# A hybrid decoder step: projection and heads in one block, a PSUM copy between two chunks, the output projection by seven products

## What is computed

```python
qa, ka, va, qb, kc, vc, ksl, vsl, kw, vw, gates = _mix_inputs(xp, norm_attn[l], w_in[l])   # RMSNorm, one projection
o_a = _dilated_prompt(qa, ka, va, bias_a)                  # 8 heads, windows (128,1), (512,4), (2048,16)
o_cmp, p_slc = _nsa_compressed(qb, _compress(kc, *cmp_k), _compress(vc, *cmp_v), pos_p, bias_b)
top_i, top_ok = _nsa_select(p_slc, pos_p)                  # 16 blocks of 64 tokens
o_slc = _nsa_selected_prompt(qb, ksl, vsl, top_i, top_ok, pos_p, bias_b)
o_win, _ = _banded_attention(qb, kw, vw, NSA_WINDOW, 1, bias_b)
o_b = _gate_branches(gates, o_cmp, o_slc, o_win)
xp, conv_p = _out_and_ffn(xp, o_a, o_b, *ffn_w, ...)       # output projection + residual, RMSNorm, up, conv, SiLU gate, down
```

## Time and profile before

| what | value |
|---|---|
| median of three runs | 2149.1 us (2150.56, 2148.54, 2149.1) |
| the profiled execution | 2152.93 us, its span 2151.2 us |
| mean granted clock of TensorE | 0.981 |
| busy PE, DVE, ACT, POOL | 2051.5, 1082.9, 521.6, 532.7 us |
| `front` | 0 to 508 us |
| `compressed_and_dilated` | 512.5 to 627 |
| `sample_selected` | 635.5 to 832 |
| `prompt_attention` | 835.6 to 1180.3 |
| `ffn`: output projection, up, down | 1182 to 1307.9, to 1864.7, to 2145 |

### The profile page before, as it was taken

One profiled execution on the slowest core, in us unless ns is written; L12 is line 12 of the kernel. 1 busy time (PEld: TensorE's weight loads), 2 busy tenths in 40 slices (PEclk: granted clock), 3 DMA queues, 4 the chain that ended last, 5 costly groups with the idle time before them and its releaser, 6 DMA issues. The chain is left out here.

```text
span 2151.2 us, 31682 instructions
## 1 busy us (share of the span) xinstructions
PE 2051.5 (95%) x12366; PEld 1339.3 (62%) x12366; DVE 1082.9 (50%) x2484; ACT 521.6 (24%) x1106; POOL 532.7 (25%) x714
## 2 busy tenths in 40 slices
PE   6999999998977997999999999999999999999998
PEld 3445466665545665666676447888888888734443
DVE  5035455411525455666776226767777765611452
ACT  4111011001323344766766111011111111000011
POOL 1444234202024551012222101222322222303110
PEclk9999999998999998999999999999999999999999
DMA  8477678643697996222251414666556622601100
GB/s 219 138 241 258 243 294 305 236 170 109 231 339 290 402 396 226 99 67 68 82 155 39 133 60 156 215 208 204 196 196 211 220 79 60 227 12 30 42 40 39
DMA packets 156393, 373.05 MB, mean 173 GB/s; under 512 B 36981, under 2 KB 95085, under 8 KB 138189
## 3 DMA queue, kind: packets, MB, share of 16 engines
q1 hardware_dynamic: 126580, 149.89, 22.2%
q0 software_dynamic: 25280, 149.44, 18.0%
q10 hardware_dynamic: 4384, 71.68, 9.5%
HBM read 343.68 MB, written 98.60 MB: 206 GB/s over the span
## 5 line engine op out<-in xcount | busy, mean ns | idle before, releaser
L2773 PE MATMUL ff_ps<-ff_hx,whole_aw 128*128 128x264 f32 x2464 | 550.5, 386 | 0.9 <-DVE ff_hx L3074 0.9
L2773 PEld LDWEIGHTS ff_ps<-ff_hx,whole_aw 128*128 128x128 f32 x2464 | 467.1, 190 | 80.8 <-issue 1.4
L802 DVE STREAM_TRANSPOSE whole_space<-whole_space 128x512 f32<-128x512 f32 x256 | 155.3, 674 | 153.7 <-PE in_psH L611 142.0
L575 PE MATMUL in_ps<-in_w,in_xT 128*128 128x512 f32 (+1 forms) x512 | 201.5, 547 | 0.0
L1155 DVE CUSTOM_DVE_ANT_0 pa_L<-pa_psS,whole_space 128x512 f32<-128x512 f32 (+3 forms) x288 | 138.9, 532 | 46.8 <-PE pa_psS L1008 45.8
L575 PEld LDWEIGHTS in_ps<-in_w,in_xT 128*128 128x128 f32 x512 | 95.0, 190 | 94.2 <-issue 87.6
L1135 ACT ACTIVATE pa_L<-pa_L,pa_nm 128x640 f32<-128x640 f32 (+3 forms) x192 | 141.9, 741 | 32.3 <-DVE pa_nm L1165 30.5
L2799 PE MATMUL ff_ps<-ff_hx,whole_space 128*128 128x512 f32 x336 | 148.0, 593 | 0.0
L700 ACT ACTIVATE in_yout<-in_ps 128x128 f32<-128x128 f32 (+5 forms) x88 | 41.0, 479 | 378.8 <-PE in_ps L575 199.6
L3155 DVE SCALAR_TENSOR_TENSOR whole_space<-whole_space,ff_kept 128x1024 f32<-128x1024 f32 x88 | 123.3, 1401 | 3.1
L611 PE MATMUL in_psH<-whole_space 128*64 128x256 f32 (+1 forms) x1152 | 121.6, 364 | 0.0
(11 more groups left out here) (411 smaller groups left out, 2579.9 us busy)
## 6 DMA issues: line engine op xcount, KB each, us to landing
out_new_a_k_s<-in_cache_a_k ACTq DMA_DIRECT2D x8, 4088.0 KB
out_new_a_v_s<-in_cache_a_v ACTq DMA_DIRECT2D x8, 4088.0 KB
whole_aw<-in_w_up SPq DMA_DIRECT2D x44, 512.0 KB
in_w<-in_w_in SPq DMA_DIRECT2D x5, 2048.0 KB
whole_space<-in_cache_a_k SPq DMA_DIRECT2D x8, 1024.0 KB
whole_space<-in_cache_a_v SPq DMA_DIRECT2D x8, 1024.0 KB
ff_hx<-in_w_down SPq DMA_DIRECT2D x14, 512.0 KB, 4.7
whole_space<-in_x_prompt SPq DMA_DIRECT2D x13, 512.0 KB, 4.0
```

The lines of the kernel that those rows point to most:

```text
L575: mm = pe.matmul(ps[0:n, b, 0:width], xT[:, k, t * P:t * P + n], w[:, at % WBUF, k, 0:width], start=(k == 0), stop=(k == KC - 1))
L802: last = dve.transpose(put[:, dh, :, k * HD:k * HD + HD].rearrange("p t (g b) -> p t g b", g=2), got[:, :, :, dh, :])
L2773: mm = pe.matmul(ps[:, bank_of(x, j, g), 0:H2], aw[:, j % 2, at, k, :], hx[:, bt, k, g * H2:g * H2 + H2], start=(k == 0), stop=(k == KH - 1))
```

## The change

**One block for two stages.** `front` and `compressed_and_dilated` share a block, its semaphores and one PSUM tensor `bank` of eight banks. Instead of the barrier, each engine waits for what it needs of the stage before (`ended`: the products, the hidden halves, the compressed copies, the evictions). The spreading copies of `QX` go from DVE to POOL, ahead of `AB`; DVE's `rep` copy goes behind its first key copies. On SP the eight stores of `mixc` go behind the loads of choice, new keys and window keys, with a semaphore of their own, on which `sample_selected` (DVE, before its first logits) and `prompt_attention` (SP) wait; the window biases are issued by ACT at the end of its program. The window keys are loaded as "b (p t) c", in pieces of 512 numbers, and put in order by strided copies out of PSUM in `sample_selected`.

**A copy between two chunks.** Where a unit s has two logits chunks and the first bank of s - 2 is one of DVE's, DVE copies that bank between the two.

**Seven products.** `mixT` of the eight prompt tiles (two halves of four tiles by two halves of the inner 1024) and the output weight (four quarters) are multiplied by seven products of quarters, in the Winograd form. Sums of the weight (T1 to T4, 128x4x512, in place) are made on DVE, those of `mixT` (S1 to S4, in place) on POOL; the first product is copied to `V` by ACT; DVE and POOL add the products into the residual rows, which are now loaded directly into nine `x1` buffers ahead of the up weights. Transposes of a tile follow one product behind.

```diff
 class Mem:
-    def __init__(self, nc, stack, stage):
+    def __init__(self, nc, stack, stage, within=None):
+        self.nc, self.stack, self.stage, self.sems = nc, stack, stage, within.sems if within else []
+        if within is None:
+            stack.callback(self.end)
...
 def front(...):
-        block = m.block()
+        ended = {"jobs": (s_pe, NJ), "half": (s_h, NR), "copied": (s_o, NR),
+                 "by_act": (s_ev[0], done(NJ - 1)[0]), "by_dve": (s_ev[1], done(NJ - 1)[1])}
...
 def prompt_attention(...):
+            def between(s):
+                return 2 <= s < U and first_bank(s - 2) is not None and chunk0[s + 1] - chunk0[s] == 2
...
             def logits(u):
+                    if x == 0 and between(u):
+                        copy_bank(u - 2, first_bank(u - 2))
...
             def copies(u):
                 for b in range(bank0[u], bank0[u + 1]):
+                    if on_dve(b) and not (between(u + 2) and b == bank0[u]):
+                        copy_bank(u, b)
...
 def compressed_and_dilated(...):
         def _(pool):
+            pool.wait_ge(*ended["copied"])
             pool.memset(QX[:, :, :, :], 0.0).then_inc(d_z, 1)
+            pool.wait_ge(d_q, 16)
+            pool.wait_ge(d_z, 1)
+            for h2 in range(2):
+                r = slice(h2 * HD, h2 * HD + HD)
+                for j in range(4):
...
+                    pool.tensor_copy(put, got).then_inc(d_qx, 1)
...
-            pre.load_window_bias(sp)
             pre.load_new_values(sp)
-            sp.wait_ge(s_st, 16 * QT)
...
+                if n == 0 and h == 0:
+                    pe.wait_ge(*ended["half"])
...
+                        pe.wait_ge(*ended["by_act"])
+                        pe.wait_ge(*ended["by_dve"])
+                        pe.wait_ge(*ended["copied"])
                         pe.wait_ge(d_rep, 1)
                         pe.wait_ge(d_ab, 2)
                         pe.wait_ge(d_qx, 8)
...
+            act.wait_ge(d_qk, 2 * NB)
+            pre.load_window_bias(act)
...
 def sample_selected(...):
-                    copy(KT[:, b // 4, b % 4, :], psT[:, u % 3, :]).then_inc(s_ca if mine else s_cd, 1)
+                    copy(KT[:, b // 4, b % 4, :].rearrange("p (n t) -> p t n", t=4),
+                         psT[:, u % 3, :].rearrange("p (t n) -> p t n", t=4)).then_inc(s_ca if mine else s_cd, 1)
...
+                        dve.wait_ge(ops.s_mixc, 16 * (SEQ // P))
...
 def ffn(...):
+            def out_products():
+                for t in range(4):
+                    out_product(2 + t, A11o[t], B11o).then_inc(s_o1, 1)
...
+                    out_product(6 + t, A12o[t], B21o).then_inc(s_o2, 1)
...
+                    out_product(10 + t, A21o[t], T12o).then_inc(s_o5, 1)
...
+                    out_product(14 + t, A12o[t], B22o).then_inc(s_o3, 1)
+                pe.wait_ge(s_ot2, 1)
...
+                    out_product(18 + t, A21o[t], T12o).then_inc(s_o6, 1)
+                    if t:
+                        transposes(t - 1)
+                pe.wait_ge(s_ot4, 1)
...
+                    out_product(22 + 2 * t, A22o[t], T4o).then_inc(s_o4, 1)
...
+                    out_product(23 + 2 * t, A21o[t], T3o).then_inc(s_o7, 1)
+                    transposes(3 + t)
...
+            for t in range(4):
+                pool.wait_ge(s_o6, t + 1)
+                pool.wait_ge(s_os4, t + 1)
+                pool.tensor_tensor(A21o[t], A22o[t], A21o[t], ALU.subtract).then_inc(s_os3, 1)
...
+                pool.tensor_tensor(x1[5 + t][:, 0:512], x1[5 + t][:, 0:512], V[t], ALU.add).then_inc(s_bl, 1)
+                pool.tensor_tensor(x1[5 + t][:, 512:D], x1[5 + t][:, 512:D], V[t], ALU.add).then_inc(s_br, 1)
...
+            def upper_rows(t):
+                if t == 0:
+                    before_upper()
+                x = x1[1 + t][:, right]
...
+                dve.tensor_tensor(V[t], ps[:, (18 + t) % 6, :], V[t], ALU.add).then_inc(s_v2, 1)
...
+                dve.tensor_tensor(x, x, V[t], ALU.add).then_inc(s_x1, 2)
+                if t == 3:
+                    dve.wait_ge(s_ot4, 1)
+                    dve.tensor_tensor(T3o, T12o, B11o, ALU.subtract).then_inc(s_ot3, 1)
...
+                dve.tensor_tensor(x[:, left], ps[:, (22 + 2 * t) % 6, :], x[:, left], ALU.add).then_inc(s_a4, 1)
...
+                dve.tensor_tensor(x[:, left], b, x[:, left], ALU.add).then_inc(s_a7, 1)
+                dve.tensor_tensor(x[:, right], b, x[:, right], ALU.add).then_inc(s_x1, 2)
```

More of the change, by code:

```diff
@@ L221, in load_bias, with front @@
             sp.dma_start(self.T[i][:, h, SEQ - back:SEQ], src).then_inc(self.s_ld[i], 16)
-def front(nc, io, scr, pre, idx, ident, kcs, vcs, s_st, s_ps):
+def front(nc, io, scr, pre, idx, ident, kcs, vcs, s_st, s_ps, joint, bank, block):
     NP = 5
@@ L892, in _ @@
             pool.wait_ge(s_ps, 32)
-    return total
+    return total, ended
 def backwards(x, tiles=1):
@@ L1203, in _, with compressed_and_dilated @@
                     finish(s - 3)
-def compressed_and_dilated(nc, io, scr, mixB, GB, Qb, pre, ident, kcs, vcs, knew, s_nl, s_mixed, stores):
+def compressed_and_dilated(nc, io, scr, mixB, GB, Qb, pre, ident, kcs, vcs, knew, s_nl, s_mixed, s_mixc, stores, ended, joint, bank, block):
     QT = SEQ // P
@@ L1416, in _ @@
                 load(i)
-            for n in range(QT):
-                half, ch = n // 4, n % 4
-                sp.wait_ge(s_o[n % 2], n // 2 + 1)
-                sp.dma_start(scr["mixc"][ch * P:ch * P + P, half * 512:half * 512 + 512], outp[n]).then_inc(s_st, 16)
             sp.wait_ge(s_out, 16)
@@ L2530, in ffn @@
         s_k4 = m.sem("stack_ready")
-        s_x = [m.sem(f"x_loaded{i}") for i in range(3)]
+        s_x = [m.sem(f"out_{name}_rows_loaded") for name in ("sample", "upper", "lower")]
+        s_o1 = m.sem("o1_in_psum")
+        s_o2 = m.sem("o2_in_psum")
+        s_o3 = m.sem("o3_in_psum")
+        s_o4 = m.sem("o4_in_psum")
+        s_o5 = m.sem("o5_in_psum")
+        s_o6 = m.sem("o6_in_psum")
+        s_o7 = m.sem("o7_in_psum")
+        s_os1 = m.sem("out_s1_ready")
+        s_os2 = m.sem("out_s2_ready")
+        s_os3 = m.sem("out_s3_ready")
+        s_os4 = m.sem("out_s4_ready")
+        s_ot1 = m.sem("out_t1_ready")
+        s_ot2 = m.sem("out_t2_ready")
+        s_ot3 = m.sem("out_t3_ready")
+        s_ot4 = m.sem("out_t4_ready")
+        s_oc = m.sem("o1_copied")
+        s_a2 = m.sem("o2_added")
+        s_a1 = m.sem("o1_added")
+        s_au = m.sem("o5_added_above")
+        s_al = m.sem("o5_added_below")
+        s_a3 = m.sem("o3_added")
+        s_v2 = m.sem("out_u2_ready")
+        s_bl = m.sem("out_u2_added_left")
+        s_br = m.sem("out_u2_added_right")
+        s_a4 = m.sem("o4_added")
+        s_a7 = m.sem("o7_added_left")
         s_cv = m.sem("conv_transposed")
@@ L2648, in up_weights @@
                                  wup[:, v, :, j * P:j * P + P]).then_inc(s_wu[j % 2], 16)
+            for i in range(1, NTILE):
+                sp.dma_start(x1[i], x_rows(order[i])).then_inc(s_x[1 + i // 5], 16)
             sp.wait_ge(s_cv, 1)
@@ L2827, in _ @@
             out_sum()
-            for i in range(1, NTILE + 2):
-                if i < NTILE:
-                    out_tile(i)
-                if i == NTILE:
-                    product("M1", 0)
-                if i >= 2:
-                    transposes(i - 2)
+            out_products()
+            product("M1", 0)
+            for i in (NTILE - 2, NTILE - 1):
+                transposes(i)
             product("M2", 0)
@@ L2960, in _ @@
             for i in range(NTILE + 2):
+                if i == 1:
+                    for t in range(4):
+                        act.wait_ge(s_o1, t + 1)
+                        nc.scalar.activation(V[t], ps[:, 2 + t, :], ACT.Copy).then_inc(s_oc, 1)
                 if i < NTILE:
@@ L3288, in hybrid_step @@
         pre = Selected(nc, Mem(nc, stack, "sel"), io, scr, idx, space)
-        total = front(nc, io, scr, pre, idx, ident, kcs, vcs, s_st, s_ps)
-        Qb = m.sb("Qb", [P, NB, 4, 2, NT])
-        mixB = m.sb("mixB", [P, NB * 32])
-        GB = m.sb("GB", [P, 3, NB * 32])
-        knew = m.sb("knew", [RS, 2, P])
-        pre.share(m.sb("turned", [P, 4096]))
-        compressed_and_dilated(nc, io, scr, mixB, GB, Qb, pre, ident, kcs, vcs, knew, s_nl, ops.s_mixed,
-                               list(zip(s_st, total)))
+        with ExitStack() as both:
+            joint = Mem(nc, both, "joint")
+            bank = joint.ps("bank", [P, 8, 512])
+            block = joint.block()
+            total, ended = front(nc, io, scr, pre, idx, ident, kcs, vcs, s_st, s_ps, joint, bank, block)
+            Qb = m.sb("Qb", [P, NB, 4, 2, NT])
+            mixB = m.sb("mixB", [P, NB * 32])
+            GB = m.sb("GB", [P, 3, NB * 32])
+            knew = m.sb("knew", [RS, 2, P])
+            pre.share(m.sb("turned", [P, 4096]))
```

(2 more changed lines are left out.)

236 lines of the change are left out of this document (165 added, 71 removed).

## The result

The changed kernel takes 2135.07 us, median of six runs, against 2149.83; the ratio to the kernel before is 0.9923, 95% interval [0.9907, 0.994]. That is 13 to 20 us less, faster as forecast (by under 1%), but about half of the 31 us forecast, and outside the stated range of 2108 to 2131. The profiled run has a span of 2132.6 us.

What follows compares the result with a forecast made beforehand. The prediction took TensorE (PE), busy 2051.5 of 2151.2 us, as the bound. Its terms 9 + 6 + 11.3 + 5 = 31.3 us came off the median 2149.1, giving 2117.8, said as 2118, range 2108 to 2131.

Steps and rivals of the forecast that it cites:

- Heads' beginning: Barrier between projection and heads: without it PE goes on sooner and the first half-step ends earlier; 9 us (6 to 11.4).
- POOL's price for the spreading copies: Eight copies moved from DVE to POOL ahead of AB: not in the trace, bounds nothing and 5.1 us, taken as 2.82.
- Heads' end: Barrier ahead of the sample stage: 7.2 us won by re-ordering SP's queue, less 1.2 for transfers; 6 us (3 to 7.2).
- part A: Front and heads in one block, queues re-ordered: 9 us at the heads' beginning and 6 at their end.
- rival 1: Sample stage becomes bound by its transfers, so the barrier's gain is only lent; 2124 to 2127 us; chance 0.15.
- a growth of over 3 us: Sample stage: growing by more than 3 us was named beforehand as something that would show the forecast wrong.
- Prompt attention: Items 0 to 7: DVE's earlier bank copy removes eight PE stalls of 1.44 us; 11.3 us (8 to 11.6).
- ACT is the next late one: Prompt attention: ACT's exponentials wait 0.69 us longer, while PE still has about 1.7 us of transposes and products.
- the 0.2 us to spare: Prompt attention: DVE's copy ends at about 887.1, PE wants the bank at 887.3, so the stall is just gone.
- rival 3: Prompt attention: the copy doesn't come earlier since DVE waits for the bank; 0 to 3 us, 2126 to 2129; chance 0.08.
- Seven products: Output projection: 13.7 us fewer PE matmuls, less waits for DVE, which POOL's SBUF lock slows; 5 us (0 to 10).
- Rival 4: Output projection: PE waits for DVE at each tile and falls to 1.2 GHz; slower, 2155.5 us; chance 0.03.

Runs made afterwards that it cites:

- b_only: The kernel before with only the bank copy between two logits chunks in the prompt attention: 2147.26 us, ratio 0.9993.
- c_only: The kernel before with only the output projection by seven products: 2143.13 us, ratio 0.9967.
- a_only: The kernel before with only front and heads in one block and the queues re-ordered: 2145.75 us, ratio 0.9981.
- a_bfix: The changed kernel with ACT copying a unit's first bank between two exponentials instead of behind both, in the prompt attention: 2124.14 us, ratio 0.9877.
- with the bias first: `a_only` with POOL's block bias additions ahead of its gathers of selected values in the sample stage: 2132.44 us, ratio 0.9919.
- the version where both are mended: `a_bfix` with POOL's block bias ahead of the gathers, and its four differences ahead of eight additions beside the sixth product: 2110.48 us, ratio 0.9815.
- mixact_bias: `a_bfix` with the eight prompt stores issued by ACT and POOL's block bias ahead of the gathers: 2114.25 us, ratio 0.9836.

## Why the prediction was right or wrong

- **Heads' beginning: right, a little small.** 10.9 us for a forecast 9 (6 to 11.4). The mis-sized part is POOL's price for the spreading copies: 1.38 us, between the bounds of nothing and 5.1, where I took DVE's 2.82. With it PE's wait is 0.27 and the doubt on the clock falls away.
- **Heads' end: wrong, nothing of the 6 us came.** I had 7.2 at the barrier less 1.2 for transfers, and both terms failed. The gap gave 3.3 in the profiled run (it is 3.1 to 6.7 us in the kernels with part A, 9.4 to 10.4 in those without), because the stores behind the window keys wait for room in SP's queue: I had priced the stores at their place in the program, not at the queue's fill, although show win_k waiting so. Without them the landing of the window keys holds PE (3.41 and 6.67 us of gap with the stores on ACT's queue); I had asked when they are issued, not when they land. And the sample stage took back not 1.2 but 3.2 in this profile and, against the 195.7 of `b_only` and `c_only`, 10 in `a_only`. This is rival 1, which I had given 0.15, and a growth of over 3 us was one of my signs of being wrong. The strided copies, which I had priced at nothing, took 0.4 to 0.5 us more each; in the stage's length that isn't seen, which with no wait for win_v is 192.7 to 195.8 us with them and 195.6 to 195.8 without. What I read wrongly is the earlier trace rows: the share of 0.62 before the stage and the wait of only 2.67 for win_v belong together, if, as argued above, the pause is what let win_v in on time. Against the rival I held that PE waits in that stage for ACT more than for DMA; that was so before, and by this account because of the pause.
- **Prompt attention: wrong, and the largest miss of the table.** 1.7 us for 11.3; the interval of `b_only` is 4 us less to 1 us more. The step that failed is "ACT is the next late one, and the unit two steps back still gives PE about 1.7 us of transposes and products to do". The stall on DVE's copy did go, with the 0.2 us to spare; the size is rival 3's (0 to 3), its cause is not. But when PE no longer stands 1.44 us, it comes to its next transposes that much earlier, while the maximum comes a copy's 0.69 us later: 2.1 us of slack were spent, and there was about 1 (ACT's 0.92 us ahead of its copies). Eight waits of 1.44 us gave way to eight of 1.05. I had set the 1.7 us against the 0.69 alone. `a_bfix` shows the rest of it: with one more copy moved, on ACT, the 11.5 us arrive.
- **Seven products: right, with the mechanism.** 7.1 us for 5 (0 to 10). The waits are at the second and third transposes and at the seventh product, as worked out, and what POOL's additions cost beside DVE is 3.6 us of the phase. PE waits 2.4, 1.0 and 1.7 us and not 4.6, 1.9 and 0.7: the scalings beside POOL took 1.6 us, the low end of the 1.6 to 2.3 that I had named, while T3 took 3.36 and not 2.36. The clock stayed at 1.00 through these waits, where I had feared a fall worth 1.7. The sum was loose besides: 13.7 less the waits of 7.2 and the 0.9 at the end is 5.6, not 5.2; measured, 13.7 less 5.1 and 0.6 is 8.0, so 0.9 us of the phase stay unplaced.
- **Rival 4** didn't come near: the lower tiles have no waits.
- **Sum.** Forecast 31; 10 of it didn't come in the attention, and some 11 of part A's 15 were held or taken back around the sample stage (4 us for part A alone, 17 with the bias first), while the products gave 2 more than forecast (the beginning's 2 more are in part A's 4). In the version where both are mended the time is 40 us below the kernel before (0.9815).

## What to carry to other kernels

When a stall is removed from the engine that sets the time, add the stall to the price of whatever comes next: that engine arrives earlier by it, and everything it meets must be early by the sum of both shifts. A pause at a barrier can be what lets a queue of transfers run dry; before taking it away, list what is queued there and who waits for the last of it, and put what is needed first ahead of what is merely allowed first. A change that shows a fraction of its gain may be held by a few lines that it doesn't touch: here two, on ACT and on POOL, were worth 11 us each.

## What the runs showed that I had not expected

- POOL made eight copies of 64x32 in 1.38 us, DVE the same ones in 2.82.
- A transfer issue can block its engine for 14.9 us (the first of the six stores in the changed kernel, the most of the 21.39 us above); nothing but transfers issued before it stands in that time. In `mixact_bias` a load of 16 KB stood 11.52 us at the same place.
- One wait, for win_v, moved the sample stage by 7 us between profiles of kernels whose program is the same there: 4.75 us of it with a stage of 199.5, 10.6 with one of 206.6. With the bias first, where nobody waits for win_v, the stage lies between 192.7 and 195.8 in six kernels.
- Waits of PE of 1.47, 0.95 and 1.72 us in the output projection left the clock at 1.00, as the 1.44 of the attention had. After the same wait of 1.90 us ahead of `ffn` it stayed at 1.00 in `a_bfix` and read 0.54 a us later in the changed kernel.
